# Hybrid decoder step on one core: five weight loads per block in place of six in the 520-column projections, two in place of three in the memory projection

## The reference

```python
mk, mv = rmsnorm(mem, g_mem) @ wk_x, rmsnorm(mem, g_mem) @ wv_x      # mem: 256 tokens
proj = rmsnorm(x, g_mix) @ w_in                                      # 2048 -> 6400
x += concat(conv3(A), retention(B), rwkv7(C), conv31(D)) @ w_out     # token mixers on proj
x += cross_attention(rmsnorm(x, g_xa) @ wq_x, mk, mv) @ wo_x
x += relu(rmsnorm(x, g_mlp) @ w_up) ** 2 @ w_down                    # width 8192
y = rmsnorm(x, g_final)
```

## Time and profile before

| | before |
|---|---|
| median of three runs | 3059.8 us (3056.35 to 3060.24) |
| span of the profiled execution | 3057.7 us |
| PE busy, share of the span | 2963.3 us, 97% |
| DVE busy | 2049.7 us, 67% |
| ACT, POOL busy | 1082.1 us, 696.3 us |

### The profile page before, as it was taken

How to read it: one execution, slowest core, us unless ns; L and a number is a source line. 1 busy time by engine, 2 the same in 40 slices (tenths; PEclk the granted TensorE clock), 3 DMA queues, 4 the chain that set the end, 5 groups by cost and what they waited for, 6 DMA issues and landing times.

```text
span 3057.7 us, 62591 instructions
## 1 busy us (share of the span) xinstructions
PE 2963.3 (97%) x27548; PEld 2898.3 (95%) x27548; DVE 2049.7 (67%) x2301; ACT 1082.1 (35%) x1244; POOL 696.3 (23%) x336
## 2 busy tenths in 40 slices
PE   8999999999988899999999899999999999999997
PEld 8999999999978799988799899999999999999997
DVE  6516975354766632322222799999999899999998
ACT  5432112223212222311232455555555433333434
POOL 6974443333300244422234000000000100000000
PEclk9999999999989999999999999999999999999998
DMA  8773533322220133365643256665566875555542
GB/s 272 222 203 91 104 104 117 97 90 91 85 85 4 46 122 122 125 214 200 217 164 118 83 177 192 205 208 192 187 196 218 321 247 201 184 198 198 206 153 91
DMA packets 236224, 485.34 MB, mean 159 GB/s; under 512 B 25136, under 2 KB 137008, under 8 KB 225968
## 3 DMA queue, kind: packets, MB, share of 16 engines
q1 hardware_dynamic: 128880, 321.79, 32.4%
q10 hardware_dynamic: 96896, 95.64, 10.1%
q0 software_dynamic: 10176, 63.90, 5.6%
HBM read 396.24 MB, written 85.03 MB: 157 GB/s over the span
## 4 chain that ended last, share of the span: by engine, by line
PE 89%; DVE 8%; issue 1%; ACT 1%; DMA 1%; ACTq 0%; DVEq 0%
PE gp L1780 36%; PE mp L1920 23%; PE gp L1920 18%; DVE work L362 2%; PE gp L976 1%; PE mp L976 1%; PE mp L1390 1%; PE mp L1407 1%; PE gp L1829 1%; DVE work L1227 1%; PE gp L1872 1%; PE mp L1438 0%; PE mp L1419 0%; DVE lo L2462 0%; DVE sums L2453 0%
## 5 line engine op out<-in xcount | busy, mean ns | idle before, releaser
L1780 PE MATMUL gp<-xh,hi 128*128 128x260 f32 x3008 | 857.7, 285 | 1.2 <-DMA work<-in_consts 1.2
L1780 PE MATMUL gp<-xh,lo 128*128 128x260 f32 x3008 | 849.7, 282 | 0.0
L1780 PE MATMUL gp<-xl,hi 128*128 128x260 f32 x3008 | 847.0, 282 | 0.0
L1729 POOL TENSOR_TENSOR lo<-raw,hi 128x1024 fp32r<-128x1024 f32 x256 | 637.9, 2500 | 852.9 <-ACT hi L2003 832.3
L2003 ACT ACTIVATE hi<-raw 128x1024 fp32r<-128x1024 f32 x260 | 274.5, 1059 | 933.7 <-PE gp L1780 865.3
L1780 PEld LDWEIGHTS gp<-xh,hi 128*128 128x128 f32 x3008 | 566.0, 188 | 12.9 <-issue 7.7
L1780 PEld LDWEIGHTS gp<-xl,hi 128*128 128x128 f32 x3008 | 565.7, 188 | 0.6
L1780 PEld LDWEIGHTS gp<-xh,lo 128*128 128x128 f32 x3008 | 565.8, 188 | 0.0
L2140 ACT ACTIVATE hi<-sums 128x1024 fp32r<-128x1024 f32 x256 | 271.2, 1059 | 340.8 <-DVE sums L2453 230.7
L1920 PE MATMUL mp<-xs,hi 128*128 128x260 f32 x2048 | 376.0, 284 | 2.8 <-issue 1.8
L1920 PE MATMUL mp<-ub,hi 128*128 128x260 f32 x2048 | 375.1, 283 | 3.6 <-DVE work L2489 3.6
(11 more groups left out here) (394 smaller groups left out, 5014.8 us busy)
## 6 DMA issues: line engine op xcount, KB each, us to landing
raw<-in_w_up SPq DMA_DIRECT2D x128, 512.0 KB, 5.0
raw<-in_w_down SPq DMA_DIRECT2D x128, 512.0 KB, 4.6
ub<-u_scratch POOLq DMA_DIRECT2D x56, 1040.0 KB, 8.5
raw<-in_w_in SPq DMA_DIRECT2D x100, 512.0 KB, 3.5
u_scratch<-uh ACTq DMA_DIRECT2D x32, 910.0 KB, 8.0
u_scratch<-ul ACTq DMA_DIRECT2D x32, 910.0 KB, 9.4
raw<-in_w_k SPq DMA_DIRECT2D x32, 512.0 KB, 4.5
raw<-in_w_v SPq DMA_DIRECT2D x32, 512.0 KB, 4.5
```

The source lines that it names most:

```text
L1729: nc.gpsimd.tensor_tensor(lo[:, s, :], raw[:, s, :], hi[:, s, :].bitcast(F32), ALU.subtract).then_inc(lo_ready, 1)
L1780: last = nc.tensor.matmul(gp[:, par, h, 0:c1 - c0], w, m[:, c0:c1], start=a, stop=b)
```

## The change

A block of a 520-column projection becomes five multiplications (`x_step`). The operands lie in one tensor `xx`: per block two pieces of 288 columns (28 columns of the low part, then a 260-column half of the high part) and one piece of 464 columns of the low part. `hi` is multiplied with 288, 464 and 288 columns, `lo` with 260 and 260; that is 1560 moving columns, as before. The low parts of the first 464 columns fall on the same 464 PSUM columns of bank 0, so columns 260 to 463 of the tile have their low share in bank 0 (`gpmid`) and the last 56 theirs in the first 28 columns of both banks (`gptail`): an eviction must add these to the main part (`gpmain`). A memory block becomes two multiplications (`mem_step`): `hi` with 512 columns (high and low part side by side) and `lo` with 256.

```diff
+XE = 28
+XW = H2 + XE
+XB = T - 2 * XE
...
+            def mem_step(par, k, wh, wl, first, final):
+                if not final:
+                    nc.tensor.matmul(gp[:, par, 0, :], wh, mm[:, :, k, :], start=first, stop=False)
+                last = nc.tensor.matmul(gp[:, par, 0, 0:NM], wl, mh[:, k, :], start=False, stop=False)
...
+            def x_step(par, k, wh, wl, first, final):
+                b0, b1 = gp[:, par, 0, :], gp[:, par, 1, :]
+                one, other, low = x_wide(k)[:, 0:XW], x_wide(k)[:, XW:], x_low(k)
+                if not final:
+                    nc.tensor.matmul(b0[:, 0:XW], wh, one, start=first, stop=False)
+                nc.tensor.matmul(b0[:, XE:XE + XB], wh, low, start=False, stop=False, skip_group_check=True)
...
+                nc.tensor.matmul(b1[:, 0:XW], wh, other, start=first, stop=False)
+                nc.tensor.matmul(b0[:, XE:XW], wl, one[:, XE:], start=False, stop=False)
+                return nc.tensor.matmul(b1[:, XE:XW], wl, other[:, XE:], start=False, stop=False)
...
-                        for h, (c0, c1) in enumerate(cols):
-                            for w, m, a, b in ((wh, xhi, kt == 0 and q == 0, False), (wh, xlo, False, False),
-                                               (wl, xhi, False, kt == UK - 1 and q == last_unit)):
-                                last = nc.tensor.matmul(gp[:, par, h, 0:c1 - c0], w, m[:, c0:c1], start=a, stop=b)
+                        last = step(par, k0 + kt, wh, wl, kt == 0 and q == 0, kt == UK - 1 and q == last_unit)
```

Every eviction gets longer. In the input projection (`evict`) one scaling operation of 520 columns becomes a copy, a wait for it, and two additions:

```diff
-            nc.vector.tensor_tensor(halves(target(n)), gphalf(n % 2), halves(rstdx[:, :]), ALU.mult).then_inc(evac, 1)
+            t, par = target(n), n % 2
+            nc.vector.tensor_copy(halves(t), gpmain(par)).then_inc(lane.sem, 1)
+            lane.n += 1
+            dve.wait_ge(lane.sem, lane.n)
+            nc.vector.tensor_tensor(mid(t), mid(t), gpmid(par), ALU.add)
+            nc.vector.tensor_tensor(tail(t), tail(t), gptail(par), ALU.add).then_inc(evac, 1)
```

```diff
             for n in range(2 * KT):
-                if n == KT + 6:
+                if n == KT + 2:
                     invert(2, T, rstdx)
-                stage_tile(n, 0, U_KV, NM, rstd)
+                for k in x_tiles(n):
+                    nc.vector.tensor_tensor(X[:, k, :], X[:, k, :], rstdx, ALU.mult).then_inc(S("x_scaled"), 1)
+                stage_tile(n, 0, U_KV, rstd)
                 if n < KT:
-                    dve.wait_ge(S("xh"), n + 1 + at("xh", "x"))
-                    nc.vector.scalar_tensor_tensor(out=xl[:, n, :], in0=X[:, n, :], scalar=pr("g_mix", n), in1=xh[:, n, :].bitcast(F32),
-                                                   op0=ALU.mult, op1=ALU.subtract).then_inc(S("xl"), 1)
                     accumulate("x", n, T)
                 if n > KT:
                     turned(n - KT - 1)
+                for k in x_tiles(n):
+                    low_of_x("x", k, "g_mix")
```

More of the change, by code:

```diff
@@ L1764, in _, with product @@
         def _(pe):
-            def product(t, par, units, u, moving, cols, ready=None, base=0, then=None, each=None):
+            def mem_step(par, k, wh, wl, first, final):
+                if not final:
+                    nc.tensor.matmul(gp[:, par, 0, :], wh, mm[:, :, k, :], start=first, stop=False)
+                last = nc.tensor.matmul(gp[:, par, 0, 0:NM], wl, mh[:, k, :], start=False, stop=False)
+                if final:
+                    last = nc.tensor.matmul(gp[:, par, 0, :], wh, mm[:, :, k, :], start=False, stop=True)
+                return last
+            def x_step(par, k, wh, wl, first, final):
[4 more added lines that the diff above has]
+                nc.tensor.matmul(b0[:, XE:XE + XB], wh, low, start=False, stop=False, skip_group_check=True)
+                if final:
+                    nc.tensor.matmul(b0[:, XE:XW], wl, one[:, XE:], start=False, stop=False)
+                    nc.tensor.matmul(b0[:, 0:XW], wh, one, start=False, stop=True)
+                    nc.tensor.matmul(b1[:, XE:XW], wl, other[:, XE:], start=False, stop=False)
+                    return nc.tensor.matmul(b1[:, 0:XW], wh, other, start=False, stop=True)
+                nc.tensor.matmul(b1[:, 0:XW], wh, other, start=first, stop=False)
+                nc.tensor.matmul(b0[:, XE:XW], wl, one[:, XE:], start=False, stop=False)
+                return nc.tensor.matmul(b1[:, XE:XW], wl, other[:, XE:], start=False, stop=False)
+            def product(t, par, units, u, step, ready=None, base=0, then=None, each=None):
                 pe.wait_ge(evac, t + 1)
@@ L1785, in product, with gemm_tile @@
                         then(q)
-            def x_moving(k):
-                return xh[:, k, :], xl[:, k, :]
-            def m_moving(k):
-                return mh[:, k, :], ml[:, k, :]
-            def u_moving(k):
-                return uh[:, k, :], ul[:, k, :]
             two = ((0, H2), (H2, T))
-            def gemm_tile(name, n, t0, u0, moving=x_moving, cols=two, then=None, each=None):
-                product(n + t0, n % 2, ((2 * (n % 2), 0), (2 * (n % 2) + 1, UK)), 2 * n + u0, moving, cols,
+            def gemm_tile(name, n, t0, u0, step=x_step, then=None, each=None):
+                product(n + t0, n % 2, ((2 * (n % 2), 0), (2 * (n % 2) + 1, UK)), 2 * n + u0, step,
                         S("xl") if n == 0 else None, at("xl", name), then, each)
@@ L1826, in part @@
                         pe.wait_ge(S("xl"), base + k + 1)
-                    for h, (c0, c1) in enumerate(two):
-                        for w, m, a, b in ((hi, xh, k == 0, False), (hi, xl, False, False), (lo, xh, False, k == KT - 1)):
-                            last = nc.tensor.matmul(gp[:, n, h, 0:H2], w[:, s, kt * P:(kt + 1) * P], m[:, k, c0:c1], start=a, stop=b)
+                    last = x_step(n, k, hi[:, s, kt * P:(kt + 1) * P], lo[:, s, kt * P:(kt + 1) * P], k == 0, k == KT - 1)
                 if n == 0 and q == 0:
@@ L1869, in out_tile @@
                 pe.wait_ge(lo_ready, U_OUT + 2 * n + q + 1)
-                for h, (c0, c1) in enumerate(two):
-                    for w, m, a, b in ((hi, xh, i == 0, False), (hi, xl, False, False), (lo, xh, False, i == KT - 1)):
-                        last = nc.tensor.matmul(gp[:, n, h, 0:H2], w[:, 2 * n + q, kt * P:(kt + 1) * P], m[:, k, c0:c1], start=a, stop=b)
+                wh, wl = (w[:, 2 * n + q, kt * P:(kt + 1) * P] for w in (hi, lo))
+                last = x_step(n, k, wh, wl, i == 0, i == KT - 1)
                 if i == UK - 1 and n == 0:
```

149 lines of the change are left out of this document (90 added, 59 removed).

## The result

The changed kernel takes 3092.6 us (median of four runs, 3089.94 to 3097.59), the kernel before beside it 3058.25 (3056.35 to 3060.24): a ratio of 1.0115, interval 1.0101 to 1.0128. It is slower, by 34 us, where 35 us less were forecast. The profiled execution took 3091.98 us, its span is 3090.2, which is 32.5 more than before.

A forecast was written before the change was run, and what follows sets the result against it. PE was taken to bound most of the kernel, DVE the stretch to L334 and 805.6:853.3. Terms -2 + 5.2 - 13.8 + 0.6 + 0.5 - 27.6 + 2.0 gave -35 us, from 3059.8 to 3025 us; range 3005 to 3052.

The forecast's parts named there:

- The sign that I had named: 520-column products: the forecast is wrong if 288 columns take 130 ns or more; 122 to 123 were expected.
- surplus of 11.3: 520-column blocks: ns per load-and-multiplication pair above its stream; if each pair keeps it, a block saves only 11.3 ns.
- the right rival: 520-column products: the rival "Pace by columns", that the surplus goes with columns streamed and not with weight loads; 3073 us.
- -27.6 over the last 46 tiles: Query, output and `wo_x` tiles: all at PE's pace, 0.60 us less a tile, so -27.6 us.
- -13.8, +0.6, +0.5: Behind the convolution, in us: tiles 19 to 44 at nine tenths of PE's gain, tiles 45 to 49, end of the mixers.
- Forecast -2: Memory stage in all: 4.2 us gained in tiles 1 to 15, +2.3 in the second half; bounds -12 and +31.
- I take 6.4, near the lower end: Memory tiles 18 to 31: DVE's loop takes 6.4 us a tile, between at least 5.9 and about 8.9.
- +5.2 forecast: Input tiles 0 to 19, up to L334: DVE sets the end, longer evictions add 8.4 us, sum +5.2 us.
- my second rival: Whole kernel: everything at PE's pace, DVE's blocked time elastic and the memory loop overlapping fully; -71 us, 2989 us; chance 0.10.
- the four joints: Stage ends, the one to the MLP among them: longer evictions and three-piece lows cost +2 us in all.
- Pace by columns: Products: surplus goes with columns, 0.46 ns each, so only DVE's additions stay; 3073 us; chance 0.11 with the 11.3 ns bound.
- the memory loop in series: Second half of the memory stage: DVE's loop runs all in series, +31 us there, 3058 us; chance 0.11.

The follow-up runs named there:

- micro1: Whole program replaced by stretches of 96 products of one kind, each with its own weight load; 256 columns start every 120.0 ns in float32r, 109.2 in bfloat16.
- ev3: The kernel before with only the input projection's evictions made three operations (520, 204, 56 columns), the two added ones adding PSUM columns a second time; 3066.34 us, ratio 1.0025.
- e2: The changed kernel with the memory projection and its eviction as before (three products of 256 columns a block, eviction in one operation); 3069.05 us, ratio 1.0038.
- low3: The kernel before with every low part of the 520-column operands written in three pieces (260, 204, 56 columns) in place of one; 3070.99 us, ratio 1.0037.
- e1p: Kernel e1 with the memory tile's eviction in three operations, none with both inputs in SBUF; 3064.92 us, ratio 1.0017.
- e1: The kernel before with the memory projection alone in two products (512 and 256 columns) and its eviction in two operations; 3074.87 us, ratio 1.0052.
- x6: The changed kernel with the 464-column product split into 260 and 204 columns, so six weight loads a block, same 1560 columns; 3129.73 us, ratio 1.0235.

## Why the prediction was wrong

**The pace, the step that failed first.** "I therefore read a floor of about 120 ns for weight load and multiplication together, and above it columns times 0.417 plus 2.6." The floor is 111.4 ns, and 260 columns lie above it; the price of a column is 0.445 ns and not 0.417. The sign that I had named came: behind 288 columns 130.6 and 132.1 ns, where 122.6 were forecast. The 0.417 came from float32 records, a form of operand that these products do not have; micro1 has float32r beside bfloat16, and the difference, 10.8 ns at 256 columns, is the "surplus of 11.3" that I gave to the weight load. The argument against the right rival, 256 and 260 columns at 120.0 and 119.6 ns, compared two stretches of different kind; back to back in micro1 they differ by 1.6 ns. (By the rival's own figures 256 columns would take 117.8 ns, not the 118.1 that I wrote.) A block saves 7.6 ns, 0.12 us a tile in place of 0.60: -5.6 in place of -27.6 over the last 46 tiles. Behind the convolution -12.7 were forecast up to the mixers' norms (-13.8, +0.6, +0.5) and -2.4 came: 30 tiles give -3.7, ev3's evictions +3.6, and the rest, -2.3, is open. The rule that I cited, N/2.4 + 2.5 ns (the Trainium skill, "TensorE: Matmul & The Clock Gate", "Back-to-back issue gap"), is met by bfloat16 in micro1, 109.2 ns for 256 columns, and missed by float32r with 120.0. The section gives it for an isolated product and not for a stream of weight loads and products; the bfloat16 stream here, with a weight load for each product, meets it all the same.

**The memory stage, the larger miss.** Forecast -2, measured +21.9. The step is "I take 6.4, near the lower end, since the loop of the first half with 7.8 us in series runs at 5.7". The loop took about 7.5 us a tile, two evictions in 15.0. With 7.5 my own sum would have said +12 for the stage. I had read that inputs in SBUF obstruct, but priced it as 0.46 us of POOL for 520 columns, in proportion to the columns. It is a wait to the end of POOL's operation, 1.9 to 2.9 us in the lines above, per operation that meets one; seven operations a tile in place of two, three of them short pieces, were therefore much dearer than their 1296 columns. Nor did I see what stands ahead of the last eviction, three low pieces and three scalings, two of the six held: a wait of 8.4 us. In e2 the same three scalings, the first started 0.05 us ahead of POOL's subtraction, take 0.70 us each; it is the subtraction that lasts 4.11 us, and PE waits 1.0 us. PE's stretches at half clock behind the waits, some 5 us, were in no term either. The first half did go as forecast: evictions 5.4 to 5.6 us apart against 5.48, and 2.8 us ahead of the kernel before at tile 16.

**Right, or right for another reason.** L334 still waits for the convolution: +5.2 forecast, +4.2 measured; but ev3 has +3.7 for 8.6 us of additions, so the elastic taps of my second rival were partly there. The eviction's price, 0.56 us, was measured as 0.57. "With the lows in three pieces ... I put +2 us for the four joints": the place is right, the cost is not. low3 measured 12.2 us for it, as VectorE's last pieces run into POOL's subtractions, which my +0.2 us a block did not contain.

**The rivals.** "Pace by columns" (3073 us) and "the memory loop in series" (+31 there) each held in part, and at once: the pace as the first had it, and much of the loss of the second, whose loop would take 8.9 us a tile and took 7.5, and not for the number of its steps. I had priced them as alternatives. The first with +22 in place of its +2.3 gives 3093, but that it meets 3092.6 is luck in part: it has +7.6 at L334 and 3.8 behind it, where 4.2 and 6.4 were measured. Sum of the measured parts: 21.9 + 4.2 - 2.4 + 8.8 = 32.5.

No version beat the kernel before: the nearest, e1p, is at 1.0017. The two-product form in memory tiles 17 to 31 of the kernel before alone, where no low part is made, would be worth 15 x 0.14 = 2 us by the pace; it was not run, as that is below what a measurement tells.

## What to carry to other kernels

Take the pace of a product from products of the same operand form, at two column counts far apart; a floor and a slope can't be told from two counts that are close. Merging moving columns pays much only where a product is at the floor; for float32r here that is under some 240 columns, an estimate from 111.4 ns at 192 and 120.0 at 256, and 260 were above it. On VectorE beside a busy GpSimd, count operations whose inputs are all in SBUF, not columns: each may last as long as GpSimd's, so don't split one in pieces without need. Keeping what releases a PSUM buffer free of them took e1 from +15.6 to +4.9, but alone gave the changed kernel 2.6 us only, as its pieces were held instead.

## What the runs showed of the hardware

- float32r products: 0.445 ns a column between 288 and 464 columns, 111.4 ns with 192 and 128; 64 columns had starts of 111 and 213 ns. bfloat16 with 256 columns 109.2, with 128 columns 55.8 ns.
- Behind a product of 204 float32r columns the next starts after 95 ns, below the 111.4, and the one after that comes 18 ns late (x6).
- A VectorE copy from SBUF to SBUF with a single input is held by GpSimd too (2.38 us in place of 0.29), and so is an operation that writes PSUM from two SBUF inputs (2.45 us).
- The order decides who is held: in e2 a scaling of VectorE that started 0.05 us ahead of GpSimd's subtraction took its 0.70 us, and so did the two behind it, while the subtraction took 4.11 us.
- GpSimd's subtraction, 2.34 us beside operations that read PSUM, takes 2.68 us where 520-column operations with SBUF inputs alternate with it.
